# Differential attention: the first query-key panel moved between the two value panels, and the first softmax component left unscaled

## What is computed

```python
qkv = x @ w_qkv                       # 8 heads, each with 2 query and 2 key components of 64, and a value of 128
q, k = rotary(q) * 64 ** -0.5, rotary(k)
lam = exp(sum(lq1 * lk1)) - exp(sum(lq2 * lk2)) + lam_init
s = einsum('bqhcd,bkhcd->bhcqk', q, k)            # c = 0, 1: the two components
s = where(mask, s, NEG_INF)                       # a query sees the keys up to the end of its chunk of 64
p = softmax(s, axis=-1)
a = p[:, :, 0] - lam * p[:, :, 1]
o = einsum('bhqk,bkhe->bqhe', a, v)
o = o * rsqrt(mean(o * o) + 1e-5) * g * (1 - lam_init)     # over the 128 values of a head, per query
return o @ w_o
```

## Time and profile before

| what | value |
|---|---|
| median of 3 runs | 2489.02 us (2488.49 to 2496.2) |
| span of the profiled execution | 2489.8 us |
| mean granted TensorE clock | 0.980 of full speed |
| busy share of PE, DVE, ACT, POOL | 95%, 40%, 36%, 38% |
| attention stage in the span | about 1268 to 1520 us |
| longest sum of PE's waits by one releaser | 16.7 us in 13 waits, for DVE's mixed rows |

### The profile page before, as it was taken

One profiled execution on the slowest core, in us unless ns is written; L12 is line 12 of the kernel. 1 busy time (PEld: TensorE's weight loads), 2 busy tenths in 40 slices (PEclk: granted clock), 3 DMA queues, 4 the chain that ended last, 5 costly groups with the idle time before them and its releaser, 6 DMA issues.

```text
span 2489.8 us, 33519 instructions
## 1 busy us (share of the span) xinstructions
PE 2372.0 (95%) x13336; PEld 1923.3 (77%) x13336; DVE 984.1 (40%) x1767; ACT 908.8 (36%) x1546; POOL 936.7 (38%) x710
## 2 busy tenths in 40 slices
PE   7999999999999979999999888999999999999997
PEld 6877787778768867877786657888888888888885
DVE  5434245246535534533215784522202354422203
ACT  4334434233434543334323443423313323332311
POOL 3423353134410003432343322555454554555544
PEclk9999999999989979999999989999999999999999
DMA  5322222032200003432222112332232233323231
GB/s 144 72 64 68 78 85 85 34 82 85 85 35 3 4 33 77 86 84 36 94 85 68 51 52 52 101 95 90 85 135 85 85 102 102 101 86 101 85 129 57
DMA packets 136739, 191.83 MB, mean 77 GB/s; under 512 B 30992, under 2 KB 84624, under 8 KB 136608
## 3 DMA queue, kind: packets, MB, share of 16 engines
q1 hardware_dynamic: 127296, 183.61, 24.9%
q10 hardware_dynamic: 9312, 6.35, 0.9%
HBM read 187.84 MB, written 2.10 MB: 76 GB/s over the span
## 4 chain that ended last, share of the span: by engine, by line
issue 56%; POOL 28%; PE 14%; DVE 1%; DMA 0%; POOLq 0%; ACT 0%; SPq 0%; DVEq 0%; ACTq 0%
POOL weights_low L659 28%; PE bank L690 5%; PE bank L692 5%; PE bank L691 5%; DMA weights_raw<-in_fox_w_in_dram 0%; POOLq L664 0%; DVE x L2327 0%; DVE x L2351 0%; POOLq L658 0%; DVE x L2325 0%; ACT weights_high L1568 0%; DVE row_statistics L2301 0%; DVE row_statistics L2359 0%; DVE xt_low L2338 0%; ACT x_normalised L1664 0%
## 5 line engine op out<-in xcount | busy, mean ns | idle before, releaser
L659 POOL TENSOR_TENSOR weights_low<-weights_raw,weights_high 128x512 fp32r<-128x512 f32 x688 | 923.6, 1373 | 1529.7 <-ACT weights_high L1568 1529.7
L690 PE MATMUL bank<-xt_high,weights_high 128*128 128x512 f32 (+1 forms) x1600 | 609.7, 381 | 10.1 <-POOL weights_low L659 6.9
L692 PE MATMUL bank<-xt_high,weights_low 128*128 128x512 f32 (+1 forms) x1600 | 598.3, 374 | 0.0
L691 PE MATMUL bank<-xt_low,weights_high 128*128 128x512 f32 (+1 forms) x1600 | 597.9, 374 | 0.0
L1568 ACT ACTIVATE weights_high<-weights_raw 128x1024 fp32r<-128x1024 f32 x344 | 344.7, 1051 | 681.0 <-PE bank L692 673.9
L690 PEld LDWEIGHTS bank<-xt_high,weights_high 128*128 128x128 f32 x1600 | 303.4, 190 | 73.6 <-POOL weights_low L659 12.2
L692 PEld LDWEIGHTS bank<-xt_high,weights_low 128*128 128x128 f32 x1600 | 302.7, 189 | 54.5
L691 PEld LDWEIGHTS bank<-xt_low,weights_high 128*128 128x128 f32 x1600 | 303.3, 190 | 49.7
L690 PE MATMUL bank<-weights_high,xt_high 128*128 128x512 f32 x512 | 206.0, 402 | 6.6 <-DVE xt_low L2338 4.9
L692 PE MATMUL bank<-weights_high,xt_low 128*128 128x512 f32 x512 | 200.8, 392 | 0.0
L691 PE MATMUL bank<-weights_low,xt_high 128*128 128x512 f32 x512 | 200.3, 391 | 0.0
(11 more groups left out here) (393 smaller groups left out, 2994.1 us busy)
## 6 DMA issues: line engine op xcount, KB each, us to landing
weights_raw<-in_fox_w_in_dram SPq DMA_DIRECT2D x64, 512.0 KB, 5.8
weights_raw<-in_ffn_w_gate_dram SPq DMA_DIRECT2D x44, 512.0 KB, 4.0
weights_raw<-in_ffn_w_up_dram SPq DMA_DIRECT2D x44, 512.0 KB, 4.9
weights_raw<-in_ffn_w_down_dram SPq DMA_DIRECT2D x40, 512.0 KB, 4.4
weights_raw<-in_gla_w_in_dram SPq DMA_DIRECT2D x24, 512.0 KB, 4.1
weights_raw<-in_gdn_w_in_dram SPq DMA_DIRECT2D x24, 512.0 KB, 4.5
weights_raw<-in_attn_w_qkv_dram SPq DMA_DIRECT2D x24, 512.0 KB, 4.3
weights_raw<-in_conv_w_in_dram SPq DMA_DIRECT2D x24, 512.0 KB, 4.5
```

The costliest lines, as they stand in the source:

```text
L659: pool.tensor_tensor(w_lo[:, odd, k], raw[:, odd, k], w_hi[:, odd, k].bitcast(F32), ALU.subtract)\
L690: pe.matmul(out_ap, lh, rh, start=first, stop=False)
L691: pe.matmul(out_ap, lh, rl, start=False, stop=False)
L692: return pe.matmul(out_ap, ll, rh, start=False, stop=last)
```

## The change

**Order of the panels.** The query-key panel of heads 0 and 1 becomes the second panel (`VALUE_PANELS`, `HEAD_PAIR`), its blocks in banks 4 to 7. The second value panel becomes the third, in banks 0 to 3. The loads follow. The first two pairs of scores wait for the values taken (`v_taken` at 6 and 8), no longer for the fourth head copy. Later query-key panels stay where they were.

**The softmax.** The first component is no longer divided by its sum s0. The second is scaled by -lambda s0 / s1 and added, so that a row of the mix is s0 times what it was. The per-row norm behind it removes that factor, once its 1e-5 is multiplied by s0 squared; s0 is kept for all pairs in `pair_norms[:, 3]`. This takes one DVE instruction out of each `mix` and adds one to each of the two batches of `mean_squares`.

The diff, cut:

```diff
 HEAD_ORDER = (0, 2, 1, 3)
+VALUE_PANELS = (0, 2)
+HEAD_PAIR = {1: 0, 3: 1, 4: 2, 5: 3}
 PAIRED = ((0, 0), (1, 0), (0, 1), (1, 1), (2, 0), (3, 0), (2, 1), (3, 1))
...
                             four = slice(HALF * odd, HALF * odd + HALF)
-                            if p < 2:
+                            if p in VALUE_PANELS:
+                                col = 2 * D + COLS * VALUE_PANELS.index(p)
                                 parts = [((slice(None), slice(2 * m, 2 * m + 2)),
-                                          w[:, HALF * odd + 2 * m:HALF * odd + 2 * m + 2,
-                                            2 * D + COLS * p:2 * D + COLS * p + COLS]) for m in range(2)]
+                                          w[:, HALF * odd + 2 * m:HALF * odd + 2 * m + 2, col:col + COLS])
+                                         for m in range(2)]
                             else:
+                                col = half * HEAD_PAIR[p]
                                 parts = [((slice(None), slice(None), slice(half * m, half * m + half)),
-                                          w[:, four, D * m + half * (p - 2):D * m + half * (p - 1)]) for m in range(2)]
+                                          w[:, four, D * m + col:D * m + col + half]) for m in range(2)]
                             load_slot(st["pair"] + p, odd, parts)
...
-                        if not odd:
-                            c = 4 * (p - 2) + pos
-                            if c < 4:
-                                pe.wait_ge(diff["v_taken"], c + 1)
-                            elif c < 6:
-                                pe.wait_ge(diff["v_taken"], 8)
-                            else:
-                                pe.wait_ge(diff["copied"], c - 1)
-                        dst = bank[pos] if p == 2 else bank[(4, 7)[pos % 2]]
+                        c = 4 * HEAD_PAIR[p] + pos
+                        if not odd and c >= 4:
+                            pe.wait_ge(diff["copied"], 4 if c < 6 else c - 1)
+                        dst = bank[4 + pos] if c < 4 else bank[(4, 7)[pos % 2]]
                         piece(st["pair"] + p, HEAD_ORDER[pos], odd, dst, False)
...
                     first_rows(st)
                     pe.wait_ge(dve_freed, st["dve"])
+                    for pos, odd in PAIRED:
+                        head_block(1, pos, odd)
                     for b, odd in PAIRED:
-                        piece(st["pair"] + 1, b, odd, bank[4 + b], True)
-                    for pos, odd in PAIRED:
-                        head_block(2, pos, odd)
+                        if not odd:
+                            pe.wait_ge(diff["v_taken"], b + 1)
+                        piece(st["pair"] + 2, b, odd, bank[b], True)
                     n_all = ATTN_HEADS * TT
-                    pe.wait_ge(diff["copied"], 4)
                     for n in range(2):
+                        pe.wait_ge(diff["v_taken"], 6 + 2 * n)
                         pair_scores(n)
...
                         wait_bank(act, st, p, b)
-                        act.activation(c_rows[:, b, COLS * p:COLS * p + COLS], bank[4 * p + b][:], ACT.Copy)\
+                        half = VALUE_PANELS.index(p)
+                        act.activation(c_rows[:, b, COLS * half:COLS * half + COLS], bank[b][:], ACT.Copy)\
                             .then_inc(diff["v_taken"], 1)
...
 
-                        c = 4 * (p - 2) + pos
+                        c = 4 * HEAD_PAIR[p] + pos
                         wait_bank(act, st, p, pos)
...
                             act.wait_ge(diff["rotated"], c)
-                        src = bank[pos] if p == 2 else bank[(4, 7)[pos % 2]]
+                        src = bank[4 + pos] if c < 4 else bank[(4, 7)[pos % 2]]
                         act.activation(rotary_in[:], src[:], ACT.Copy).then_inc(diff["copied"], 1)
...
                             src = bank[SCORE_BANKS[score_slot(n)][c]]
+                            total = soft[:, 6 + k:7 + k] if c else pair_norms[:, 3, n:n + 1]
                             act.activation(pair_probs[:, n % 2, c, 0:keys], src[:, 0:keys], ACT.Exp,
-                                           bias=soft[:, k:k + 1], accum_out=soft[:, 6 + k:7 + k])\
+                                           bias=soft[:, k:k + 1], accum_out=total)\
                                 .then_inc(diff["exps"], 1)
...
-                    for p in range(2):
-                        take_value(p, 0)
-                        take_value(p, 1)
-                        weights_high(st["pair"] + p + 1, 0)
-                        take_value(p, 2)
-                        take_value(p, 3)
-                        weights_high(st["pair"] + p + 1, 1)
-                    take_head(2, 0)
-                    take_head(2, 1)
+                    take_value(0, 0)
+                    take_value(0, 1)
+                    weights_high(st["pair"] + 1, 0)
+                    take_value(0, 2)
+                    take_value(0, 3)
+                    weights_high(st["pair"] + 1, 1)
+                    take_head(1, 0)
+                    take_head(1, 1)
+                    weights_high(st["pair"] + 2, 0)
+                    take_head(1, 2)
+                    weights_high(st["pair"] + 2, 1)
+                    take_head(1, 3)
+                    take_value(2, 0)
+                    take_value(2, 1)
                     weights_high(st["pair"] + 3, 0)
-                    take_head(2, 2)
+                    take_value(2, 2)
+                    take_value(2, 3)
                     weights_high(st["pair"] + 3, 1)
-                    take_head(2, 3)
                     n_all = ATTN_HEADS * TT
...
                         dve.wait_ge(diff["exps"], 2 * n + 2)
                         k = 2 * score_slot(n)
-                        link(dve.reciprocal(soft[:, 12 + k:14 + k], soft[:, 6 + k:8 + k]))
-                        link(dve.tensor_tensor(soft[:, 18 + k:19 + k], soft[:, 13 + k:14 + k], neg_lam, ALU.mult))
+                        link(dve.reciprocal(soft[:, 13 + k:14 + k], soft[:, 7 + k:8 + k]))
+                        link(dve.scalar_tensor_tensor(soft[:, 18 + k:19 + k], soft[:, 13 + k:14 + k],
+                                                      pair_norms[:, 3, n:n + 1], neg_lam, ALU.mult, ALU.mult))
                         p0, p1 = [pair_probs[:, n % 2, c, 0:(n % TT + 1) * P] for c in range(2)]
-                        link(dve.tensor_scalar(p1, p1, soft[:, 18 + k:19 + k], None, ALU.mult))
-                        dve.scalar_tensor_tensor(p0, p0, soft[:, 12 + k:13 + k], p1, ALU.mult, ALU.add)\
+                        dve.scalar_tensor_tensor(p0, p1, soft[:, 18 + k:19 + k], p0, ALU.mult, ALU.add)\
                             .then_inc(diff["mixed"], 1)
...
 
-                        c, h = 4 * (p - 2) + pos, 2 * (p - 2) + pos // 2
+                        c, h = 4 * HEAD_PAIR[p] + pos, 2 * HEAD_PAIR[p] + pos // 2
                         dst, scale = (buf_b[:, h], 1.0) if pos % 2 else (buf_a[:, h], 64 ** -.5)
...
                     def mean_squares(batch):
 
-                        u = pair_norms[:, 0, (0, 28)[batch]:(28, 32)[batch]]
+                        u, w, total = [pair_norms[:, m, (0, 28)[batch]:(28, 32)[batch]] for m in (0, 2, 3)]
+                        link(dve.scalar_tensor_tensor(w, total, LN_EPS, total, ALU.mult, ALU.mult))
                         dve.wait_ge(diff["sums"], (7, 8)[batch])
-                        dve.tensor_scalar(u, u, 1.0 / P, LN_EPS, ALU.mult, ALU.add).then_inc(diff["means"], 1)
+                        dve.scalar_tensor_tensor(u, u, 1.0 / P, w, ALU.mult, ALU.add).then_inc(diff["means"], 1)
```

2 lines of the change are left out of this document (1 added, 1 removed).

## The result

| | before | after |
|---|---|---|
| median of the runs | 2490.26 us (4 runs, 2488.49 to 2496.2) | 2473.52 us (4 runs, 2470.82 to 2476.82) |
| ratio | | 0.9931 (0.9919 to 0.9943) |
| span of the profiled execution | 2489.8 us | 2475.0 us |
| mean granted clock | 0.980 | 0.982 |

The account below looks back on a forecast made before the run. PE was taken to be bound by waiting, chiefly 16.7 us for DVE's mixed rows where POOL splits weights. Terms 5.0 - 0.2 + 0.4 + 4.0 + 3.7 + 2.7 + 1.0 = 16.6 us gave 2472.4 us, range 2466 to 2480.

Parts of the forecast that it names:

- start, to pair 0: Start of the attention loop: first transposes at 1342.1 in place of 1347.1, 5.0 us gained, ends 3.2 and 6.8.
- loss in the second value panel: Second value panel: POOL's slices come late beside the rotations, a loss of 0.2 us, ends 0 and 1.3.
- pair 3, pairs 7 to 9: Shorter mixes in the loop: 0.4 us at pair 3, 4.0 at pairs 7 to 9, the latter with ends 2.0 and 5.3.
- pairs 15 to 17: Same pattern as pairs 7 to 9, a wait of 2.20 and smaller ones: 3.7 us gained, ends 2.0 and 5.0.
- pairs 23 to 25: Last POOL split: 2.7 us gained, counted at pair 25, whose rotation and maxima keep their length; ends 1.9 and 4.
- pairs 26 to 31: Last pairs, DVE, ACT and PE waiting in turn: six scalings sum to 2.5 us, 1.0 taken, ends 0 and 2.7.
- The small product: DVE's single-column product in each mix: claimed to keep its size and number; put at 1.2 us at the start.
- rival B: Loop and start: the small product escapes POOL's first slice, PE sets the start; about 22 us gained, 2467; chance 0.12.
- rival A: Loop around POOL's splits: the wait moves from the mix to the rotation; 11.6 us gained, 2477.4; chance 0.20.
- `mean_squares`: The extra instruction there, about 0.2 us on 28 columns, is hidden by ACT's copy of the last pair's rows.
- Rival C: Loop: PE waits for ACT's exponentials, not DVE's mix and maxima, so only the start pays; 2483.8; chance 0.07.
- D: Loop: shorter, more evenly spread waits hold PE at half speed; with ten such pieces about 2499, slower; chance 0.03.

Follow-up runs that it names:

- e3: The kernel before without the scaling of the second component in pairs 7 and 15 alone; 2487.44 us, ratio 0.9991 to before.
- e2: The kernel before with only the new softmax, panels in their old order; 2480.77 us, ratio 0.9958 to before.
- e1: The kernel after with the softmax of before, so only the panel order is changed; 2492.5 us, ratio 1.0006 to before.
- e5: The kernel before with POOL's subtraction replaced by a fill with zeros, all but one column of every second slice; 2454.54 us in one run.
- e9: e1 again, unchanged, for a second profile; 2487.49 us in one run.
- e11: The kernel after with pair 0's exponentials ahead of the last `weights_high` and 18 thrown-away matmuls in PE's wait at pair 25; 2472.68 us, ratio 0.9925 to before.
- e10: e1 with thrown-away matmuls filling PE's waits at pairs 0, 7, 9, 15, 17, 23 and 24; 2490.3 us, ratio 0.9998 to before.

## Why the prediction was right, and where not

The sum was right, 16.6 against 16.7 us in the medians and 17.2 in the stage. Each term came out within 0.4 us of its size. By terms, measured at PE's transposes and counted from the first `x`, in us:

| term | forecast | measured |
|---|---|---|
| start, to pair 0 | 5.0 | 4.99 |
| loss in the second value panel | 0.2 | 0.24, one wait; within the row above |
| pair 3, pairs 7 to 9 | 0.4 + 4.0 | 4.57 (83.88 - 78.89 = 4.99 at pair 0, 131.72 - 122.16 = 9.56 at pair 9) |
| pairs 15 to 17 | 3.7 | 3.64 (175.07 - 161.87 = 13.20 at pair 17) |
| pairs 23 to 25 | 2.7 | 3.09 (219.00 - 202.71 = 16.29 at pair 25) |
| pairs 26 to 31 | 1.0 | 0.95 (17.24 at `D`) |

- **The start** was right in its chain. Within it two sizes were off and cancelled: counted from the first `x`, `weights_high` started 0.35 us later than put (73.79 for 73.44) and the small product took 0.77 for 1.2. PE was ready 0.7 later than put, so its wait is 1.20 rather than 1.9. The low end of this term should have been 3.1, not 3.2: 5.0 less 0.4 for the longer product and 1.5 for half speed.
- **The value panel** cost what was put, and no load was late.
- **Pairs 7 and 15**: the wait of 2.20 shrank by 1.40 (forecast 1.5), and the transposes to the next piece by 1.56 (forecast 1.55).
- **The small product does not keep its size.** The forecast said that it does. On one column and without POOL it takes 0.22 us, where the one before took 0.16. No wait grows by it.
- **Pairs 8 and 9**: the time is right, the reason half so. Mix(8) lost not only the scaling but the stretching of the other two instructions, since it ran ahead of POOL's second split. PE at full speed brings DVE the scores sooner: in before DVE waited 2.58 us for them there, in after 1.54. This is rival B's mechanism, without its size, because PE can't use more than its wait of 0.71. The rotation behind it was stretched instead (rival A's mechanism); in after it costs a wait of 0.38 at pair 9, in e3 one of 2.32.
- **Pair 25** did not keep its wait: 5.10 for 3.54. From pair 24's transposes PE needs 3.62 us to be ready for pair 25, at full speed, where it needed 5.50 at half speed. DVE's rotation and maxima take as long as before, so from pair 24's transposes to pair 25's it takes 8.72 us for 9.04, and the rest of what PE won became waiting. The term as a whole was 2.7 for 3.09.
- **`mean_squares`**: the added instructions took 0.18 and 0.16 us, and PE's wait before the first transposes of `D` is 0.71 as before: hidden, as put.
- **Rival C** fell with e2 and with the waits; **D** with clocks of 1.00 at pairs 7 and 15.
- **What the sum did not test**, and what the experiments show not to hold, is that the parts can be priced one by one. The price of the start, 4.8, already had the scaling of mix(0) gone; e1, which keeps it, was expected to give 3.5 to 4.8 and has 3.75 at pair 0, but at `D` 0.5 and in the timed runs nothing. The scalings at pairs 7 and 15 were priced at 1.5 + 1.55 each. Both halves of this did come at pair 7 in e3, but 1.4 us went to the wait at pair 9, and of 6.1 us the stage kept 0.55. Half speed was priced as if it belonged to one wait. It can follow any wait of 2 us and more that is left, so that what one part gains may be spent behind the next wait of that kind. Both parts together leave no such wait before pair 25. That is why the sum held, and the forecast did not look for it.

Not settled: why the same wait of 2.2 us brings half speed in one execution and none in another, and how much of e5's gain is POOL's shorter work and how much its not reading.

## What to carry to other kernels

When PE waits for an engine, price a saving on that engine by the waits that are left behind it. Here two edits gave 0.5 and 13 us of the stage alone and 17 together, because the first one's gain lasted only where no waits of 2 us were left behind it to bring half speed. A product that DVE has beside POOL's subtractions costs about a slice of POOL, not its own length: 1.28 us for a scaling of 128 columns that takes 0.29 alone. The maxima, which read PSUM, the reciprocals and the shuffles keep their lengths there. So removing a product is worth most there, and the next one may inherit the wait. Where run-to-run scatter is 3 us, gauge a small edit by marks inside the profiled stage, and time it as well before calling it a gain.

## What the runs showed of the hardware

- **Half speed behind waits of 2 us.** Single waits of 0.80 and 1.20 in after have a clock of 1.00 behind them; those of 3.37, 4.26, 5.06 and 5.10 all have half speed. In between it goes either way: 2.20 at pair 7 has full speed behind it in e1 (1371 to 1392: 1.00) and half speed in before, and pair 23's 2.2 has it in e1 and not in e9. Over all runs, nine of sixteen waits of 2.19 to 2.22 us at pairs 7, 15 and 23 have half speed behind them, while one of 2.66, at the start of e5, has 1.00. Nor is a short wait safe: e11 falls behind 0.93. Small waits close together can bring it too, as in the last pairs of e10; before has the same waits there at a clock of 1.00.

```profile
1490.00:1498.00 8.00, 5.55 (x24) 4.59 (x25) 5.11 (x16) 4.29 (x10) 0.00 (x0) 0.59 0.00 0
```

- **What a fall costs depends on who is late anyway.** Behind pair 0 in e1 it costs 1.55 us. Within pairs 7 to 9 it costs 1.0: 13.21 us with it in before, 12.19 without it in e1, since DVE's rows for pair 9 come no sooner.
- **Half speed that goes at one place can come at another.** It was 20 to 31 us in every kernel with the old softmax and POOL's subtractions, whichever waits were taken out, but for 18 in e10. In e3 the falls behind pairs 7 and 15 are gone, and others stand behind pairs 17, 23 to 25 and in the last pairs: 30.7 us in all, for 23.9 in before.
- **Which of DVE's instructions POOL stretches.** Beside POOL's subtractions of 1.26 us, a small product of one column took up to 1.18 us for 0.16 alone, a last product of 128 columns up to 1.38 for 0.35, one of 512 columns up to 1.74 for 0.75: about 1.0 us more in each, whatever the size.
